# Splitting the second unit's weights of a stage ahead of the stage change, in a two-block transformer kernel on one core

## The reference, cut to what matters

```python
h = rms_norm(x, mix_norm_g[i]) * (1.0 + sc1) + sh1
y = conformer_conv(h, ...)      # layer 0;  moba_attention(h, ...) in layer 1
x = x + g1 * y
h = rms_norm(x, mlp_norm_g[i]) * (1.0 + sc2) + sh2
x = x + g2 * (jnp.square(jax.nn.relu(h @ mlp_w1[i])) @ mlp_w2[i])
```

## Time and profile before

| | |
|---|---|
| median of 3 runs | 1301.22 us (1300.7 to 1302.53) |
| the profiled execution, its own time | 1301.9 us |
| its span, first to last instruction | 1300.1 us |
| mean granted TensorE clock | 0.975 of full speed |
| PE busy | 1210.5 us, 93% of the span |
| DVE, ACT, POOL busy | 69%, 42%, 5% |
| instructions | 20616 |

### The profile page before, as it was taken

How to read it: one execution, slowest core, us unless ns; L and a number is a source line. 1 busy time by engine, 2 the same in 40 slices (tenths; PEclk the granted TensorE clock), 3 DMA queues, 4 the chain that set the end, 5 groups by cost and what they waited for, 6 DMA issues and landing times.

```text
span 1300.1 us, 20616 instructions
## 1 busy us (share of the span) xinstructions
PE 1210.5 (93%) x8774; PEld 1096.2 (84%) x8774; DVE 892.1 (69%) x1318; ACT 545.6 (42%) x713; POOL 68.5 (5%) x73
## 2 busy tenths in 40 slices
PE   2788889999999988999999999999999999999896
PEld 2766689999999877999999999888888888888676
DVE  6974587677678664797876774775866763775744
ACT  2322456554444355564545522323212221554762
POOL 0410000000000012000000000000000000000640
PEclk8888999999999989999999999999999999999899
DMA  9599066777777540476675544332443333141000
GB/s 380 211 312 299 22 259 228 291 270 270 270 292 293 209 179 26 165 264 227 241 264 183 188 164 161 125 135 97 162 162 130 132 128 122 70 158 66 1 2 33
DMA packets 37788, 233.64 MB, mean 180 GB/s; under 512 B 4656, under 2 KB 9008, under 8 KB 10432
## 3 DMA queue, kind: packets, MB, share of 16 engines
q1 hardware_dynamic: 35136, 229.99, 48.1%
q10 hardware_dynamic: 2560, 2.33, 0.7%
HBM read 226.60 MB, written 1.05 MB: 175 GB/s over the span
## 4 chain that ended last, share of the span: by engine, by line
PE 73%; DVE 13%; ACT 6%; DMA 4%; issue 4%; SPq 1%; ACTq 1%; POOL 0%; DVEq 0%
PE prod L1407 22%; PE prod L1409 21%; PE prod L1408 21%; DVE w_lo L858 3%; ACT w_hi L512 3%; DMA raw<-stream 3%; DVE raw L891 2%; PE misc L1364 2%; PE misc L1515 1%; PE prod L1600 1%; DVE rows L963 1%; PE prod L1395 1%; DVE rows L885 1%; PE misc L1612 1%; DMA FH<-V 1%
## 5 line engine op out<-in xcount | busy, mean ns | idle before, releaser
L858 DVE TENSOR_TENSOR w_lo<-raw,w_hi 128x2048 fp32r<-128x2048 f32 x138 | 322.0, 2334 | 292.3 <-ACT w_hi L512 292.3
L512 ACT ACTIVATE w_hi<-raw 128x2048 fp32r<-128x2048 f32 x138 | 264.1, 1914 | 509.9 <-PE prod L1409 479.7
L1407 PE MATMUL prod<-XH,w_hi 128*128 128x256 f32 (+1 forms) x1360 | 423.9, 312 | 18.7 <-DVE w_lo L858 8.1
L1409 PE MATMUL prod<-XH,w_lo 128*128 128x256 f32 (+1 forms) x1360 | 416.9, 307 | 0.0
L1408 PE MATMUL prod<-XL,w_hi 128*128 128x256 f32 (+1 forms) x1360 | 416.7, 306 | 0.0
L1407 PEld LDWEIGHTS prod<-XH,w_hi 128*128 128x128 f32 x1360 | 262.8, 193 | 36.9 <-DVE w_lo L858 9.6
L1408 PEld LDWEIGHTS prod<-XL,w_hi 128*128 128x128 f32 x1360 | 262.9, 193 | 11.2 <-issue 0.7
L1409 PEld LDWEIGHTS prod<-XH,w_lo 128*128 128x128 f32 x1360 | 262.6, 193 | 10.9
L1407 PE MATMUL prod<-FH,w_hi 128*128 128x256 f32 (+1 forms) x640 | 195.4, 305 | 1.2 <-DVE w_lo L858 1.2
L1409 PE MATMUL prod<-FH,w_lo 128*128 128x256 f32 (+1 forms) x640 | 194.7, 304 | 0.0
L1408 PE MATMUL prod<-FL,w_hi 128*128 128x256 f32 (+1 forms) x640 | 194.7, 304 | 0.0
(11 more groups left out here) (227 smaller groups left out, 1233.5 us busy)
## 6 DMA issues: line engine op xcount, KB each, us to landing
raw<-stream SPq DMA_DIRECT2D x210, 1024.0 KB, 4.9
FH<-V SPq DMA_DIRECT2D x16, 71.0 KB, 6.3
FH<-V ACTq DMA_DIRECT2D x16, 71.0 KB, 5.4
FL<-V SPq DMA_DIRECT2D x16, 71.0 KB, 3.5
FL<-V ACTq DMA_DIRECT2D x16, 71.0 KB, 3.4
X<-x_features SPq DMA_DIRECT2D x1, 1024.0 KB, 11.2
V<-cond_rows SPq DMA_DIRECT2D x1, 1024.0 KB, 7.9
C<-ctx_features SPq DMA_DIRECT2D x1, 1024.0 KB, 6.9
```

Source lines behind the costliest of these rows:

```text
L512: A(w_hi[:, w % SPLITS, :, :].rearrange("p k c -> p (k c)"), raw[:, n % RING, :], ACT.Copy).then_inc(weight_hi, 1)
L858: tt(w_lo[:, w % SPLITS, :, :].rearrange("p k c -> p (k c)"), raw[:, n % RING, :], w_hi[:, w % SPLITS, :, :].rearrange("p k c -> p (k c)") ...
L1407: mm(out, lhs_hi, rhs_hi, start=start, stop=False)
L1409: return mm(out, lhs_lo, rhs_hi, start=False, stop=stop)
```

## The change

Three units, 13, 45 and 61 (`AHEAD`), are the second units of the three stages. Their two parts now go to a half of `FH` and `FL` in place of `w_hi` and `w_lo`, and `split_hi` of them waits for `unit_done` of unit `w - 5` in place of `w - 2`. On DVE `split_lo` of these three now comes before the drain of the last unit of the stage that ends (`LAST`: units 11, 43 and 59). The three `LAST` units also raise `half_done` after their output tile i = 0, and the drains of that tile wait for it. `KEEP_BUSY` goes from 10 to 9 products at the three changes.

```diff
-KEEP_BUSY = {0: 6, CONV_OUT: 16, MLP0: 10, QKV: 10, MLP1: 10, MIX_B: 8}
+AHEAD = {MLP0 + 1: 1, QKV + 1: 0, MLP1 + 1: 1}
+LAST = [MLP0 - 1, QKV - 1, MLP1 - 1]
+KEEP_BUSY = {0: 6, CONV_OUT: 16, MLP0: 9, QKV: 9, MLP1: 9, MIX_B: 8}
...
+        def halves(w):
+
+            if w in AHEAD:
+                c = UNIT * AHEAD[w]
+                return [m[:, c:c + UNIT].rearrange("p (k c) -> p k c", k=KT) for m in (FH, FL)]
+            return w_hi[:, w % SPLITS], w_lo[:, w % SPLITS]
...
                 if w >= SPLITS:
-                    act.wait_ge(unit_done, w - SPLITS + 1)
-                A(w_hi[:, w % SPLITS, :, :].rearrange("p k c -> p (k c)"), raw[:, n % RING, :],
+                    act.wait_ge(unit_done, w - 4 if w in AHEAD else w - SPLITS + 1)
+                A(halves(w)[0].rearrange("p k c -> p (k c)"), raw[:, n % RING, :],
                   ACT.Copy).then_inc(weight_hi, 1)
...
-                act.wait_ge(unit_done, w + 1)
+                if w in LAST:
+                    act.wait_ge(half_done, LAST.index(w) + 1)
+                else:
+                    act.wait_ge(unit_done, w + 1)
...
+                        if w in LAST and i == 1:
+                            act.wait_ge(unit_done, w + 1)
...
-                    dve.wait_ge(unit_done, w + 1)
                     j = u[-1]
                     for i in range(2):
                         k = 2 * j + i
+                        if w in LAST and i == 0:
+                            dve.wait_ge(half_done, LAST.index(w) + 1)
+                        else:
+                            dve.wait_ge(unit_done, w + 1)
...
-                if s - 1 == A_OUT_2 or s > 1 and s - 1 in FIRST_OF_SET:
+                early = s - 1 == A_OUT_2 or s > 1 and s - 1 in FIRST_OF_SET and s not in AHEAD
+                if early:
                     drain(s - 2)
...
-                if s >= 2:
-                    if s - 1 != A_OUT_2 and s - 1 not in FIRST_OF_SET:
-                        drain(s - 2)
+                if s >= 2 and not early:
+                    drain(s - 2)
...
+                        if w in LAST and (i, k) == (0, KT - 1):
+                            ins.then_inc(half_done, 1)
                 ins.then_inc(unit_done, 1)
```

More of the change, by code:

```diff
@@ L355, in build @@
         unit_done = sem("unit_done")
+        half_done = sem("half_done")
         cond_loaded = sem("cond_loaded")
@@ L857, in split_lo @@
                 dve.wait_ge(weight_hi, w + 1)
-                tt(w_lo[:, w % SPLITS, :, :].rearrange("p k c -> p (k c)"), raw[:, n % RING, :],
-                   w_hi[:, w % SPLITS, :, :].rearrange("p k c -> p (k c)").bitcast(F32),
+                hi, lo = halves(w)
+                tt(lo.rearrange("p k c -> p (k c)"), raw[:, n % RING, :],
+                   hi.rearrange("p k c -> p (k c)").bitcast(F32),
                    ALU.subtract).then_inc(unit_consumed, 1)
@@ L1418, in unit @@
                     pe.wait_ge(drained[who], n)
-                wh, wl = w_hi[:, w % SPLITS], w_lo[:, w % SPLITS]
+                wh, wl = halves(w)
                 s = FIRST_OF_SET.get(w)
```

## The result

| | before | changed |
|---|---|---|
| median of 7 runs | 1300.7 us (1298.96 to 1302.53) | 1304.17 us (1303.6 to 1306.91) |
| ratio | | 1.0034, 95% interval 1.0022 to 1.0046 |
| span of the profiled execution | 1300.1 us | 1304.7 us |
| mean granted clock | 0.975 | 0.975 |

The change makes the kernel slower by 0.34%, 4.4 us by the ratio, with 2.9 to 6.0 us inside its interval, and 3.5 us by the medians. That is clear of no change, and on the side that was forecast. The seven executions of the changed kernel lie in two groups, four at 1303.6 to 1304.2 us and three at 1306.5 to 1306.9; the profiled one, 1306.5 us, is of the second.

What follows compares the result with a forecast made beforehand. PE is busy 93% of the span; around the change to unit 44, unit 45's split ends last. Order 2.9 plus clock falls 1.4 on 1301.9 us made 1306.2, less 0.7 to the median: 1305.5 us, range 1302.3 to 1307.9.

Steps and rivals of the forecast that it cites:

- The earlier wait: ACT's high part of units 45 and 61 starts about 1.2 us earlier, behind the squares; no gain at unit 12.
- The order on DVE: Low part ahead of the updates of `x` delays the variance: 1.0 us at units 44 and 60, 0.9 at 12.
- The half signal: Saves nothing: the DVE instruction waiting for it stands behind the low part, when both halves are long done.
- one product fewer: Unread products on PE at the three changes: nine in place of ten cost or give nothing by themselves.
- the buffers: Splits written to other tiles of the same shape and kind: nothing taken for it.
- Falls of the clock: PE's longer idle stretches ahead of the last sums lower its clock: two falls of three, 0.7 us each, 1.4 us.
- The upper bound of 1.2 a fall: At the three changes, the most a clock fall was to cost; three such falls gave 3.6 us.
- the rule that I set beside it from the Trainium skill: Warns only of idle gaps longer than those at units 44 and 60; unit 12 alone falls, 0.7 us not 1.4.
- The sum: Whole kernel: 1301.9 + 2.9 + 1.4 = 1306.2 us, forecast as 1305.5 since the profiled run lay 0.7 above the median.
- Order as said, clock held: Rival: DVE's order costs 2.9 us and the clock does not fall, 1304.1 us; chance 0.20.
- Absorbed later: Rival: the delay vanishes in a later PE wait, such as at 574.08, 1301 to 1302 us; chance 0.14 with no effect.
- The splits come forward: Rival: ACT makes unit 45's high part during unit 43, similarly elsewhere; 6.2 us saved, 1295.0 us; chance 0.12.

Runs made afterwards that it cites:

- act_ahead: Changed kernel, with ACT splitting the high part of units 13, 45 and 61 one step earlier, ahead of the squares; 5.5 us faster than before (0.9958).
- bridged: Changed kernel plus unread products ahead of the last sums, 7 at unit 12 and 4 at units 44 and 60; 2.7 us slower than before (1.0021).
- drain_first: Changed kernel, but DVE drains the stage's last unit before the second unit's low part, as before the change; 3.4 us faster than before (0.9974).
- order_alone: Kernel before, with only DVE's low part moved ahead of the last unit's drain at the three changes; 8.6 us slower than before (1.0066).
- half_signal_alone: Kernel before, with only `half_done` and the waits on it added; no difference, ratio 1.0001.
- ten_unread: Changed kernel with ten unread products in place of nine at the three changes; 4.6 us slower than before (1.0035).
- low_part_in_halves: As act_ahead, with the three units' low part in two instructions, one on each side of the drain; 7.3 us faster than before (0.9944).

## Why the prediction was right

**The earlier wait gains 1.2 us at two places and nothing at unit 12.** Right: the high part follows the squares by 0.66 us in the changed kernel at units 44 and 60 (376.81 to 377.47), with no idle time, and at unit 12 as before. In act_ahead, where it goes ahead of the squares, it starts 0.1 us before DVE even reaches unit 44's low part, so the squares were what held it.

**The order on DVE costs 1.0, 1.0 and 0.9.** Right: 1.07, 1.07 and 0.95 in bridged, where the clock is out of it; 1.07 at unit 44 of the changed kernel. drain_first and order_alone show it from both sides. This is the part of the forecast that was worked out and not guessed, and 2.9 to 3.1 us of the loss rest on it.

**The half signal saves nothing, one product fewer nothing, the buffers nothing.** Right for the first two by half_signal_alone and ten_unread. For the buffers, drain_first bounds it: the instructions into `FH` and `FL` take 1.90 and 2.29 us, as those into `w_hi` and `w_lo` do.

**Falls of the clock, two of three at 0.7.** Two of three fell in the profiled execution, at units 12 and 60. They cost 0.7 at unit 12 (0.2 of it on the variance, 0.5 on the unread products behind it) and 0.9 at unit 60 (10.82 less bridged's 9.89), so 0.7 was right at one and a little low at the other. The upper bound of 1.2 a fall was too low: falls in order_alone and ten_unread put PE's first product 2.3 us later. Which of the stretches fall was a guess, and I gave the shorter two equal odds without grounds: over the changed kernel, order_alone and ten_unread the stretch of 3.5 us was followed by a fall in five cases of five, that of 2.3 in one of four. By the rule that I set beside it from the Trainium skill (TensorE: Matmul & The Clock Gate, "Why this matters for your kernels"), which warns only of longer gaps, none of those four would have been followed by a fall. One was, at unit 60 of the changed kernel. So neither the rule nor my even odds is borne out by four cases, and that the count came to two of three in the profile is luck.

**The sum.** 2.9 + 1.4 = 4.3 forecast. The ratio gives 4.4. The distances to the variance give 4.2, but they leave out the 0.5 us on the unread products at unit 12. With it PE's first products come 4.8 us later in all. The column of four units gives 4.4, since 0.3 us is made up behind unit 12. The time forecast was 1305.5 us, in a range of 1302.3 to 1307.9, and the median is 1304.17.

**The rivals.** *Order as said, clock held* gave 1304.1, and that is nearer to the median than the forecast is. The profile shows two falls, but it is of the slower three of seven executions. What the clock costs in the others no profile shows; their mean granted clock, 0.975 to 0.977 against 0.972 to 0.975, leaves room for fewer falls. So the 2.9 us is shown, and the 1.4 us is shown for one execution only. *Absorbed later* is out: from unit 16 to unit 44 the changed kernel took 161.3 us, as before, and PE's wait at 574.08 us is 2.90 us long in both. *The splits come forward* did not happen in the changed kernel, and for the reason given, the squares ahead on ACT. With ACT's order changed as well it does happen, but for less than the 6.2 us worked out: 3.9 us in act_ahead and 5.4 in low_part_in_halves, by the distances. At unit 12 the prediction's terms (183.0 + 0.5 + 0.46 + 0.47 + 0.6) add to 185.0 and not to 185.6. The 185.6 comes out with the whole 1.13 us of the last sums, and low_part_in_halves saved 2.33 us there, not 2.8.

## What to carry to other kernels

A looser wait helps only as far as the instructions ahead of it on its own engine let it through. Before moving one, find what the engine is doing at the moment when the wait would open; here it was squares that themselves waited for another engine. At full clock the change lost 3.1 us with the split behind them (bridged) and gained 3.9 with it ahead (act_ahead), on the same order of DVE. And when an instruction is put ahead of another to use the time it frees, work out which of the two the critical work needs: 2.2 us of weights for the second unit went ahead of 0.9 us that the first unit was waiting for.

## What the runs showed of the hardware

The same idle stretch of TensorE, 2.3 us between sums with the same work on either side, was followed by a granted clock of 0.50 at one place and 1.00 at three (units 44 and 60 of the changed kernel and of ten_unread), so a single profile does not tell what such a stretch costs. Two other idle stretches of PE, which no kernel here changed, say the same over all ten profiles: the one of 2.90 us (574.08 in the kernel before) was followed by a granted clock of 0.50 in eight of ten, and the one of 2.58 us (1156.98) in six of ten. The first, in the kernel before, was followed by 0.50; in drain_first it was not:

```profile
568.98:571.88 2.90, 0.00 (x0) 1.00 0.40 85
571.88:575.90 4.02, 4.02 (x33) 1.00 1.01 418
```

A low stretch also costs differently by what it falls on: on the sums of squares it delayed the variance by 0.9 us, on the unread products behind them PE's first product by 0.5. And it can be bridged: with 4 to 7 unread products in the idle stretch, which left 0.5 to 0.6 us of it, the granted clock stayed at 1.00 at all three changes in the profile of bridged.
